# Whole-block transposes in the expert stage, and the first loads of x and weights in turn behind idle matmuls

## What is computed

```python
for i in range(DEPTH):                       # DEPTH = 2
    if i % 2 == 0:
        h = x @ ev_w_in[j]                   # 2048 x 4176, split into q, kv, rope key, GLA parts
        mix = concat([mla(...), gla(...)]) @ ev_w_out[j]
    else:
        h = gelu(x @ od_w_in[j])             # 2048 x 4096
        mix = spatial_gating(h, ...) @ od_w_out[j]
    x = layer_norm(ALPHA * x + mix, ...)
    ffn = grouped_moe(x, ...)                # 16 experts, top 2 of one group
    x = layer_norm(ALPHA * x + ffn, ...)
# an expert: h = silu(t @ w_gate) * (t @ w_up);  y += combine * (h @ w_down)
```

## Time and profile before

| | |
|---|---|
| runs | 1626.01, 1627.89, 1630.12 us; median 1627.89 |
| profiled execution | 1631.01 us, of which the span is 1629.1 us |
| mean granted TensorE clock | 0.991 |
| DMA over the span | 527.45 MB, mean 324 GB/s |

### The profile page before, as it was taken

One profiled execution on the slowest core, in us unless ns is written; L12 is line 12 of the kernel. 1 busy time (PEld: TensorE's weight loads), 2 busy tenths in 40 slices (PEclk: granted clock), 3 DMA queues, 4 the chain that ended last, 5 costly groups with the idle time before them and its releaser, 6 DMA issues.

```text
span 1629.1 us, 19539 instructions
## 1 busy us (share of the span) xinstructions
PE 1554.6 (95%) x8002; PEld 917.6 (56%) x8002; DVE 701.7 (43%) x1004; ACT 455.7 (28%) x594; POOL 9.5 (1%) x19
## 2 busy tenths in 40 slices
PE   7999999999999999899889999999999999999994
PEld 6888887885353343343348888887434335344332
DVE  5444577635333332333247474463444233233325
ACT  5334466424020111011035453342311102111102
POOL 0010000000000000000000000000000000000000
PEclk9999999999999999999999999999999999999998
DMA  9565243558999999999997555446999999999996
GB/s 351 191 199 223 91 143 150 192 193 334 413 428 428 427 427 429 428 428 428 423 399 286 193 197 181 155 155 239 369 414 426 430 425 391 417 427 427 428 422 241
DMA packets 51174, 527.45 MB, mean 324 GB/s; under 512 B 5612, under 2 KB 6188, under 8 KB 12691
## 3 DMA queue, kind: packets, MB, share of 16 engines
q1 hardware_dynamic: 49874, 522.27, 78.7%
q0 software_dynamic: 1216, 4.02, 0.8%
HBM read 524.17 MB, written 2.10 MB: 323 GB/s over the span
## 4 chain that ended last, share of the span: by engine, by line
PE 77%; DMA 18%; DVE 3%; ACT 1%; SPq 1%; issue 0%; DVEq 0%; ACTq 0%
PE bank L1289 27%; DMA w_all<-in_moe_w_down 18%; PE bank L821 10%; PE bank L823 10%; PE bank L822 10%; PE bank L1247 4%; PE bank L1359 2%; PE bank L1341 1%; PE bank L1449 1%; PE bank L1260 1%; DMA w_land<-in_ev_w_in 1%; PE bank L833 1%; PE bank L1031 0%; PE bank L1033 0%; PE bank L1032 0%
## 5 line engine op out<-in xcount | busy, mean ns | idle before, releaser
L1289 PE MATMUL bank<-w_all,xg 128*64 128x512 f32 x2016 | 449.8, 596 | 16.8 <-DMA w_all<-in_moe_w_gate_up 15.9
L1289 PEld LDWEIGHTS bank<-w_all,xg 128*64 128x64 f32 x2016 | 138.3, 137 | 294.7 <-issue 258.7
L821 PE MATMUL bank<-w_hi,T_hi 128*128 128x512 f32 x736 | 291.0, 395 | 3.5 <-DVE w_lo L2096 2.6
L2096 DVE TENSOR_TENSOR w_lo<-w_land,w_hi 128x2048 fp32r<-128x2048 f32 (+1 forms) x96 | 211.9, 2216 | 182.6 <-ACT w_hi L1649 182.5
L823 PE MATMUL bank<-w_hi,T_lo 128*128 128x512 f32 x736 | 287.7, 391 | 0.0
L822 PE MATMUL bank<-w_lo,T_hi 128*128 128x512 f32 x736 | 287.4, 391 | 0.0
L1649 ACT CAST w_hi<-w_land 128x2048 fp32r<-128x2048 f32 (+1 forms) x100 | 184.0, 1852 | 222.7 <-PE bank L823 219.5
L2643 DVE TENSOR_TENSOR y_lo<-bank,y_hi 128x512 fp32r<-128x512 f32 x54 | 37.4, 692 | 430.6 <-ACT y_hi L1895 430.6
L2654 DVE SCALAR_TENSOR_TENSOR X<-bank,weight,X 128x512 f32<-128x512 f32 x224 | 152.4, 743 | 48.8 <-PE bank L1359 48.8
L821 PEld LDWEIGHTS bank<-w_hi,T_hi 128*128 128x128 f32 x736 | 138.7, 188 | 34.9 <-DVE w_lo L2096 3.4
L823 PEld LDWEIGHTS bank<-w_hi,T_lo 128*128 128x128 f32 x736 | 138.6, 188 | 29.0
(11 more groups left out here) (359 smaller groups left out, 1336.1 us busy)
## 6 DMA issues: line engine op xcount, KB each, us to landing
w_all<-in_moe_w_gate_up SPq DMA_DIRECT2D x124, 2048.0 KB, 17.5
w_all<-in_moe_w_down SPq DMA_DIRECT2D x56, 2048.0 KB, 20.7
w_land<-in_ev_w_in SPq DMA_DIRECT2D x32, 1024.0 KB, 4.9
w_land<-in_od_w_in SPq DMA_DIRECT2D x32, 1024.0 KB, 4.9
w_land<-in_ev_w_out SPq DMA_DIRECT2D x16, 1024.0 KB, 4.8
w_land<-in_od_w_out SPq DMA_DIRECT2D x16, 1024.0 KB, 4.8
w_all<-in_moe_w_down SPq DMA_DIRECT2D x12, 1024.0 KB, 24.3
w_land<-in_att_w SPq DMA_DIRECT2D x7, 1024.0 KB, 4.8
```

The costliest lines, as they stand in the source:

```text
L821: pe.matmul(dst, hi_l, hi_r, start=start, stop=False)
L1289: ins = pe.matmul(dst[halves[h], :], cols(c), U.weights(q, pos + h)[:, c, :], start=start and c == 0, stop=stop and c == 3)
L2096: dve.tensor_tensor(w_lo[:, 4 * h + j, w], w_land[:, 4 * h + j, w], w_hi[:, j, w], ALU.subtract) \
```

## The change

It has two parts.

**Start.** x's quarters and the first full block's units are loaded in turn, unit 0 as two halves of 512 KB. The tail follows as one load of 640 KB into a place of its own, so that it becomes the second block of work (`SB_TAIL = 1`) and is computed after the first full block, into bank 4; its two transposes go behind block 7. ScalarE and VectorE split unit 0 in four pieces, unit 1 in two (`FIRST_PIECES`), and TensorE takes the first block with the 128-row tile outside and the token halves inside. VectorE clears 384 columns of `X` first; on these TensorE runs 4 float32 matmuls of 256 columns at once, one when x's first quarter has landed and one when the first half unit has; ScalarE copies one column of it before its first wait.

**Turns.** `turn` transposes a whole 128 x 128 block at a time: 4 transposes into bank 6, with the 64 columns of gate and the 64 of up side by side. `silu` and `product` read bank 6 with a step of 128 columns. The wide expert's extra four matmuls go to bank 7. The branch for overflowing experts keeps the old form.

```diff
 IN0_FULL = 8
-SB_IN0, SB_OUT0 = 0, 9
+SB_TAIL, SB_OUT0 = 1, 9
...
+FIRST_PIECES = ([slice(NB * c, NB * (c + 1)) for c in range(4)], [slice(2 * NB * c, 2 * NB * (c + 1)) for c in range(2)])
...
+        if sb == SB_TAIL:
+            group.append(None)
+            before.append(0)
+            continue
-            g = sb % 2
+            g = 1 if sb == 0 else sb % 2
...
+        tail_at = b_at + 4 * (W_IN + 1536)
+        tail_land = sb("tail_land", [P, 4, 4 * TAIL], offset=tail_at)
+        tail_lo = sb("tail_lo", [P, 4, 4 * TAIL], F32R, offset=tail_at)
+        tail_hi = sb("tail_hi", [P, 4, 4 * TAIL], F32R, offset=tail_at + 64 * TAIL)
...
             for j in range(4):
                 sp.dma_start(x0T[:, 4 * j:4 * j + 4, :], A["xT"][:, 4 * j:4 * j + 4, :]).then_inc(xT_in[j], 16)
-                load(0, j, A["ev_w_in_tail"][j], n=TAIL)
-            for j in range(4):
-                load(1, j, unit(w_in0, 0, j))
+                if j == 0:
+                    for c, done in ((0, first_in), (2, landed[1][0])):
+                        sp.dma_start(w_land[:, 4, c * NB:(c + 2) * NB], unit(w_in0, 0, 0)[:, c * NB:(c + 2) * NB]) \
+                            .then_inc(done, 16)
+                else:
+                    load(1, j, unit(w_in0, 0, j))
+            sp.dma_start(tail_land[:], A["ev_w_in_tail"]).then_inc(tail_in, 16)
             sp.dma_start(const[:], A["const"]).then_inc(ident_in, 16)
...
+            def blank(n):
+
+                for _ in range(n):
+                    pe.matmul(bank[7][:, 0:2 * P], X[:, 0, 0:P], X[:, 0, P:3 * P], start=True, stop=True)
+
+            pe.wait_ge(blank_set, 1)
+            blank(4)
+            pe.wait_ge(xT_in[0], 16)
+            blank(1)
+            pe.wait_ge(first_in, 16)
+            blank(1)
             for j in range(4):
-                pe.wait_ge(t_low, 2 * j + 2)
-                wait_low(pe, 0, j)
+                if j:
+                    pe.wait_ge(t_low, 2 * j + 2)
+                for c in range(4):
+                    if j == 0 and c in (0, 2):
+                        pe.wait_ge(t_low, c // 2 + 1)
+                    if j == 0 and c < 3:
+                        pe.wait_ge(first_low, c + 1)
+                    elif j == 1 and c == 0:
+                        pe.wait_ge(first_low, 4)
+                    elif c == (3, 2, 0, 0)[j]:
+                        wait_low(pe, 0, j)
+                    t = 4 * j + c
+                    for a in range(TT):
+                        ins = three(bank[2 + a][:], xT_hi[:, t, a * P:(a + 1) * P], xT_lo[:, t, a * P:(a + 1) * P],
+                                    hi(j)[:, c, :], lo(j, 1)[:, c, :], t == 0, t == KT - 1)
+                ins.then_inc(used, 1)
+            for j in range(4):
+                wait_low(pe, SB_TAIL, j)
+                w_high, w_low = (w[:, j, :].rearrange("p (c n) -> p c n", c=4) for w in (tail_hi, tail_lo))
                 for c in range(4):
                     t = 4 * j + c
-                    ins = three(bank[0][0:TAIL, 0:SEQ], hi(j, TAIL)[:, c, :], lo(j, 0, TAIL)[:, c, :], xT_hi[:, t, :],
-                                xT_lo[:, t, :], t == 0, t == KT - 1)
+                    ins = three(bank[4][0:TAIL, 0:SEQ], w_high[:, c, :], w_low[:, c, :], xT_hi[:, t, :], xT_lo[:, t, :],
+                                t == 0, t == KT - 1)
                 ins.then_inc(used, 1)
-            gemm_block(1, 1)
-
+            with pe.Fori(1, IN0_FULL // 2) as i:
+                for p in range(2):
+
+                    pe.wait_ge(gemm_out_a, 2 * i + p - 1)
+                    pe.wait_ge(gemm_out_v, 2 * i + p - 1)
+                    gemm_block(2 * i + p, p, low=lambda j: 8 * i + (4 * p + j + 1))
             pe.wait_ge(ident_in, 16)
-            pe.wait_ge(gemm_out_a, 1)
+            pe.wait_ge(tail_out, 1)
             for a in range(TT):
                 ins = pe.transpose(bank[7][:, a * ROPE:(a + 1) * ROPE], tailT[0:ROPE, a * P:(a + 1) * P],
                                    const[0:ROPE, 0:ROPE])
             ins.then_inc(kr_filled, 1)
-            with pe.Fori(1, IN0_FULL // 2) as i:
-                for p in range(2):
-
-                    pe.wait_ge(gemm_out_a, 2 * i + p - 1)
-                    pe.wait_ge(gemm_out_v, 2 * i + p - 1)
-                    gemm_block(2 * i + p, p, low=lambda j: 8 * i + (4 * p + j + 1))
             pe.wait_ge(gemm_out_a, IN0_FULL - 1)
...
-                            for h in range(2):
-                                ins = pe.matmul(bank[6 + h][:, c * CAP:(c + 1) * CAP], gu_s[halves[h], c * P:(c + 1) * P],
-                                                const[halves[h], halves[h]], start=True, stop=True)
+                            ins = pe.transpose(bank[6][:, c * P:(c + 1) * P], gu_s[:, c * P:(c + 1) * P], ident)
                         if is_wide(layer, q, e):
                             for c in range(4):
-                                ins = pe.matmul(bank[6][:, (4 + c) * CAP:(5 + c) * CAP], gu_x[:, c * P:(c + 1) * P],
+                                ins = pe.matmul(bank[7][:, c * CAP:(c + 1) * CAP], gu_x[:, c * P:(c + 1) * P],
                                                 cst("quarters"), start=True, stop=True)
...
+            act.wait_ge(blank_set, 1)
+            act.copy(spare[0], X[:, 0, 0:1])
             for j in range(4):
                 act.wait_ge(xT_in[j], 16)
-                act.copy(xT_hi[:, 4 * j:4 * j + 4, :], x0T[:, 4 * j:4 * j + 4, :]).then_inc(t_high, 2)
-                split(0, n=TAIL, js=[j])
+                if j == 0:
+                    for t in (0, 2):
+                        act.copy(xT_hi[:, t:t + 2, :], x0T[:, t:t + 2, :]).then_inc(t_high, 1)
+                else:
+                    act.copy(xT_hi[:, 4 * j:4 * j + 4, :], x0T[:, 4 * j:4 * j + 4, :]).then_inc(t_high, 2)
+                if j >= 2:
+                    split(0, js=[j])
+                for m, v in enumerate(FIRST_PIECES[j] if j < 2 else ()):
+                    if j == 0 and m == 0:
+                        act.wait_ge(first_in, 16)
+                    elif (j, m) in ((0, 2), (1, 0)):
+                        act.wait_ge(landed[1][j], 16)
+                    act.copy(w_hi[:, j, v], w_land[:, 4 + j, v]) \
+                        .then_inc(hi_done if m + 1 == len(FIRST_PIECES[j]) else first_high, 1)
+            act.wait_ge(tail_in, 16)
+            for j in range(4):
+                act.copy(tail_hi[:, j, :], tail_land[:, j, :]).then_inc(hi_done, 1)
             def in0_out(b, half):
                 act.wait_ge(used, 4 * b + 4)
                 act.copy(H[:, 0, bass.ds((b - 1) * NB, NB)], bank[2 * half][:]).then_inc(gemm_out_a, 1)
-            split(1)
-            act.wait_ge(used, 4)
-            act.copy(tailT[:], bank[0][0:TAIL, 0:SEQ]).then_inc(gemm_out_a, 1)
+            act.sem_inc(gemm_out_a, 1)
             with act.Fori(0, IN0_FULL // 2 - 1) as i:
                 for p in range(2):
-                    split(2 * i + (p + 2), h=p, count=i + 1)
+                    split(2 * i + (p + 2), h=p, count=i + p)
                     in0_out(2 * i + (p + 1), (p + 1) % 2)
+            act.wait_ge(used, 8)
+            act.copy(tailT[:], bank[4][0:TAIL, 0:SEQ]).then_inc(tail_out, 1)
...
-                        ins = act.activation(gsil[:, :, 0:CAP], bank[6][:, 0:4 * CAP].rearrange("p (c s) -> p c s", c=4),
+                        ins = act.activation(gsil[:, :, 0:CAP], bank[6][:].rearrange("p (c s) -> p c s", c=4)[:, :, 0:CAP],
...
+            dve.memset(X[:, 0, 0:3 * P], 0.0).then_inc(blank_set, 1)
             for j in range(4):
-                dve.wait_ge(t_high, 2 * j + 2)
-                v = (slice(None), slice(4 * j, 4 * j + 4))
-                dve.tensor_tensor(xT_lo[v], x0T[v], xT_hi[v], ALU.subtract).then_inc(t_low, 2)
-                split(0, n=TAIL, js=[j])
+                for k in range(2 if j == 0 else 1):
+                    n = 2 if j == 0 else 4
+                    v = (slice(None), slice(4 * j + n * k, 4 * j + n * k + n))
+                    dve.wait_ge(t_high, k + 1 if j == 0 else 2 * j + 2)
+                    dve.tensor_tensor(xT_lo[v], x0T[v], xT_hi[v], ALU.subtract).then_inc(t_low, n // 2)
+                if j >= 2:
+                    split(0, js=[j])
+                for m, v in enumerate(FIRST_PIECES[j] if j < 2 else ()):
+                    if m + 1 == len(FIRST_PIECES[j]):
+                        dve.wait_ge(hi_done, j + 1)
+                    else:
+                        dve.wait_ge(first_high, 3 * j + m + 1)
+                    dve.tensor_tensor(w_lo[:, 4 + j, v], w_land[:, 4 + j, v], w_hi[:, j, v], ALU.subtract) \
+                        .then_inc(lo_done_v if m + 1 == len(FIRST_PIECES[j]) else first_low, 1)
+            for j in range(4):
+                dve.wait_ge(hi_done, 4 * SB_TAIL + j + 1)
+                dve.tensor_tensor(tail_lo[:, j, :], tail_land[:, j, :], tail_hi[:, j, :], ALU.subtract) \
+                    .then_inc(lo_done_v, 1)
...
```

(22 more changed lines are left out.)

7 lines of the change are left out of this document (3 added, 4 removed).

## The result

The changed kernel takes 1620.08 us (median of 5 runs, 1618.26 to 1622.32) against 1628.79 (5 runs, 1626.01 to 1631.02) for the kernel before: ratio 0.9949, 95% interval 0.9936 to 0.9962. That is some 8.3 us less, where 6.7 was forecast. Run again later beside the same kernel before, it gave 1622.38 (7 runs) against 1627.89 (30 runs), ratio 0.9964 (0.9951 to 0.9977), some 5.9 us. The profiled execution took 1620.08 against 1631.01, its span 1618.3 against 1629.1.

What follows compares the result with a forecast made beforehand. Weight streaming bounds the expert stages, TensorE the dense ones. Start 4.9 us plus turns 1.8 us make 6.7 us, from 1627.89 to 1621.2 us; range 1617.0 to 1625.5.

Steps and rivals of the forecast that it cites:

- the queue's release: Slot releases that SP awaits with an empty queue: three late ones, at 421.81, 1185.90 and 1382.12, coming 5.5, 6.1 and 6.7 us earlier.
- the third turn that it counts: The turn at 1352.19, ahead of the wide expert's late release, counted at 0.60 us saved.
- Landings: Arrival of the start's reordered loads: half unit 7.6 us, unit 1 13.3, unit 2 17.15, unit 3 20.9.
- the term for the head: Load rate at the queue's beginning: 4.7 us a MB up to 1.21 MB, then 2.55 up to 3.80, then 2.37.
- The rival of late landings: The four 512 KB loads at the head are slow, 4.7 us a MB: start 3.0, turns 1.8, 1623.1 us; chance 0.15.
- First piece: Half unit landed at 7.6 plus ScalarE and VectorE copies: TensorE begins the first block at 8.9 us instead of 19.25.
- Which landing decides: In the first block unit 2, landed 17.15 and ready at 21.4 us, ends the wait whether TensorE's clock is warm or cold.
- Between tail and block 2: ScalarE's write of `w_hi[0]` waits for the tail's first unit, making TensorE wait about 0.1 us before block 2.
- The start in all: Block 2 starts at 38.0 instead of 43.18: 5.2 us, less 0.27 later, a gain of 4.9 us.
- The two moved transposes: The tail's two transposes come behind block 7 and cost 0.27 us there.
- Idle matmuls and table load: At the start, the load's 1.28 us are worth nothing more by themselves; the sum doesn't ask whether idle matmuls raise the clock.
- Turns: 0.60 us saved per turn, 32 turns; only three, ahead of late releases, count, together 1.8 us (bounds nothing to 2.6).

Runs made afterwards that it cites:

- The run with the tail between: Changed kernel with the tail's weights loaded in four 160 KB loads, one behind each quarter of x: 1625.75 us in one run, block 2 at 40.49.
- the other old starts: Profiles of the kernel before again, with only the new turns, and with extra idle matmuls around the router: block 2 at 41.37, 41.20 and 41.87 us.
- the start alone: Changed kernel with the old turns (8 half-block matmuls into banks 6 and 7): 1623.92 us (12 runs), ratio to before 0.9976.
- the fill: Extra idle matmuls in TensorE's idle stretches ahead of both layers' first gathers: kernel before 1626.67 us, ratio 0.9993; changed kernel 1617.55 us, ratio to before 0.9939.
- the turns alone: Kernel before with only the new turns (4 whole-block transposes into bank 6): 1624.53 us (12 runs), ratio to before 0.9981.

## Why the prediction was right, and where not

The forecast of 1621.2 us is 1.1 above the first median and 1.2 below the second; the start moved block 2 through the landing that it names, and the first turn of each layer counts through the queue's release, as it says. That the sum came out is partly luck: the start is worth up to 1 us less than forecast, the third turn that it counts is worth 0.1, the first two carry more than their price, and 1.3 us of clock is not in the sum at all. By its steps:

- **Landings.** Half unit 6.3 instead of 7.6, unit 1 12.0 instead of 13.3, unit 2 16.1 instead of 17.15, unit 3 19.9 instead of 20.9. Each was 1.0 to 1.3 us early, because the term for the head was mis-sized: 4.7 us a MB came from a trace in which 160 KB loads stood between x's quarters. The run with the tail between shows that these cost 2.2 us at the head, of which 0.4 is a share for their bytes. The rival of late landings is out; half-megabyte loads did not slow the head.
- **First piece.** 7.77 instead of 8.9. With the half unit there at 6.3 it is no longer last: its first cast ends near 6.9, and VectorE's low part of x at 7.0, as forecast.
- **Which landing decides.** Unit 2, as forecast: 20.5 instead of 21.4. That the sum doesn't ask for the clock holds within 0.3 us as a mean, over eight profiles with the new start (36.95 to 37.61).
- **Between tail and block 2** a wait of 0.1 was forecast. The last tail matmul starts at 36.93 and they are 0.12 apart, so the wait is 0.3, behind ScalarE's 1.92 and VectorE's 2.30 on `w_hi[0]`; block 2 would otherwise start near 37.05.
- **The start in all**: 5.8 us against 4.9 in the two profiles, but the kernel before was profiled in an execution whose first block ran low. Against the other old starts it is 4.0 to 4.6, and the start alone measured 3.9 us. The 4.9 was sized against a 43.18 that is not typical; the early landings hid that. The two moved transposes were priced at 0.27, and the stretch behind block 2 is 0.5 longer. So at `gu_s` 0 the 5.8 us are 5.2, and with the first turn's 0.45 the first release came 5.6 us earlier, near the forecast 5.5 although each term was off.
- **Idle matmuls and table load**: nothing, as taken, for the matmuls. For the activation "worth nothing more by itself" was right of the copy, for a reason that I did not have: the load moves ahead without it.
- **Turns.** 0.45 us where the turn stands alone and 0.65 with the slots behind it, for 0.60 taken: the transposes take 0.41 to 0.59 in place of 0.44, and the slot matmuls behind them lost a delay. Two of the three places were right, the first turn of each layer. The third, ahead of the wide gather, failed: the sum took the last landing ahead of it as fixed, but with the stream earlier and the turn shorter the next landing of down weights comes last, and TensorE waits for it. The first two were mis-sized: 0.9 and 1.5 us instead of 0.60 each, since their dips reach over two windows and the prediction read one. A further 0.8 to 1.1 us behind the wide gather has no shown cause. The stages' sum is 0.9 + 1.6 + 1.1 = 3.6 us; the forecast had 1.8.
- **What the prediction missed**: 1.3 us in front of layer 1's experts, where nothing was edited. It is clock, as the fill shows. Why the kernels with new turns kept the full level there in 8 of 8 profiles and those with old ones lost it in 3 of 3, with the same instructions and idle stretches just ahead, I can't say; putting back three of the turns did not bring the loss back. That it follows from the turns is not shown.

By medians the parts add up to 3.9 + 3.1 = 7.0 us, between the 8.3 and the 5.9 measured for the whole. The stages claim more than the medians bear: 3.6 and 1.3 make 4.9 us for the turns, where the turns alone measured 3.1 (1.6 to 4.7). Each profile is one execution, and that of the turns alone, 1622.90, was faster than the median of its kernel, 1624.53.

## What to carry to other kernels

Before a saving is priced from one profile, look at the granted clock of that stretch: here one profile in four of the same start fell to the low level, and that alone was 1.2 to 1.9 us. In a streaming stage count a shortened step only where the transfer queue stands empty for it, look at the whole dip, and ask whether a landing comes last once the step is shorter: 2 of 32 turns carried the gain of two stages, and a third, expected to, gave 0.1 us. And where a short wait precedes a dense run of matmuls, a few idle ones in it can be worth more than a shorter instruction.

## What the runs showed that I had not expected

- Small loads at the head of a queue cost more than their bytes: 160 KB in front of the first half unit moved its landing by 2.2 us, and the rate between 4 and 6 us fell from 385 to 290 GB/s.
- Behind idle stretches of 0.33 and 1.02 us, with matmuls of 16 columns between them, 13 of 22 gathers ran 7 or 8 pairs of matmuls low, 0.43 us a pair instead of 0.24, beginning 0 to 1.3 us into the gather. 1.24 us of idle time inside a stream did no such thing.
- In the kernel without idle matmuls the first unit ran at 0.43 us a matmul from 7.82 on, while its window from 8 to 10 us shows a granted clock of 1.00. The pace of the records is the safer reading of the clock there.
- A table load can stand ahead of a wait that comes before its first activation (nine profiles with the new start), or behind it (four with the old one). Which it is belongs to the kernel, but no run shows what in it decides.
